# Computing the gate half of the FFN's causal convolution with vector taps instead of banded matmuls

## The reference

```python
def conv_ffn(h, w_up, conv_f_w, w_down):
    u = jnp.einsum("bsd,df->bsf", h, w_up)          # 1024 -> 2 x 2816 channels
    u = causal_dwconv(u, conv_f_w)                  # 3 taps along the sequence, per channel
    gate, val = jnp.split(u, 2, axis=-1)
    return jnp.einsum("bsf,fd->bsd", jax.nn.silu(gate) * val, w_down)
...
for l in range(2):
    h = rmsnorm(x, mix_norm_g[l]);  x = x + token_mixer(h, ...)
    h = rmsnorm(x, ffn_norm_g[l]);  x = x + conv_ffn(h, ...)
return rmsnorm(x, final_norm_g)
```

## Time and profile before

| | |
|---|---|
| two timed runs | 3695.23 and 4191.18 us (median 3943.21) |
| the profiled execution | 3684.81 us, span 3683.8 us on its slowest core |
| spans of the eight cores | 3662.6 to 3683.8 us |
| granted TensorE clock, mean of each core | 0.984 to 0.989 |
| busy share of the span | TensorE 94%, VectorE 51%, ScalarE 28%, GpSimd 17% |

### The profile page before, as it was taken

The page is one execution under the profiler, slowest core; times in us unless marked ns, Lnnn a source line. Parts: engine busy times, 40 slices in busy tenths (PEclk is TensorE's granted clock), DMA queues, the critical chain, the costliest instruction groups (busy, mean ns, idle before and its releaser), DMA issues.

```text
span 3683.8 us, 52643 instructions; the slowest of 8 cores (3662.6 to 3683.8 us)
## 1 busy us (share of the span) xinstructions
PE 3449.2 (94%) x15712; PEld 1534.9 (42%) x15712; DVE 1872.0 (51%) x3110; ACT 1043.6 (28%) x1943; POOL 626.8 (17%) x778
## 2 busy tenths in 40 slices
PE   0888699998999999999999999999999999999997
PEld 0333234443444444444444444444444444444443
DVE  1353233336575566557543333343657566666664
ACT  0322123333232223223213333333323322322321
POOL 2360000001132122123110000000222212211311
PEclk9989999999999999999999999999999999999998
DMA  9859977663454454444446667644444555455454
GB/s 157 267 191 232 180 173 185 179 176 129 155 158 140 153 161 138 151 157 155 140 154 176 176 176 181 175 142 141 130 152 158 162 169 179 140 172 174 156 162 136
DMA packets 148206, 606.76 MB, mean 165 GB/s; under 512 B 14656, under 2 KB 14784, under 8 KB 146976
## 3 DMA queue, kind: packets, MB, share of 16 engines
q1 hardware_dynamic: 130720, 519.49, 44.9%
q0 software_dynamic: 14096, 77.60, 11.2%
q10 hardware_dynamic: 3120, 6.29, 0.7%
HBM read 618.00 MB, written 83.89 MB: 191 GB/s over the span
## 4 chain that ended last, share of the span: by engine, by line
PE 82%; DMA 4%; issue 4%; DVE 4%; ACT 3%; ACTq 2%; another core or an unknown queue 0%; DVEq 0%; SPq 0%
PE ps L270 82%; ACTq L223 2%; DMA ring<-sA 2%; DMA ring<-sCA 2%; ACT stg L475 1%; DVE stg L535 1%; DVE stg L533 1%; DVE stg L481 1%; DVE hbuf L441 0%; ACT stg L537 0%; ACT L527 0%; DVE ps L439 0%; ACT stg L488 0%; DVE xs L571 0%; ACT sd L527 0%
## 5 line engine op out<-in xcount | busy, mean ns | idle before, releaser
L270 PE MATMUL ps<-hbuf,ring 128*128 128x512 bf16 x8192 | 1857.5, 382 | 90.8 <-DVE stg L481 39.4
L270 PE MATMUL ps<-stg,ring 128*128 128x512 bf16 x7072 | 1626.1, 381 | 29.0 <-DMA ring<-sCA 11.5
L270 PEld LDWEIGHTS ps<-hbuf,ring 128*128 128x128 bf16 x8192 | 800.2, 98 | 1087.4 <-issue 151.9
L270 PEld LDWEIGHTS ps<-stg,ring 128*128 128x128 bf16 x7072 | 691.0, 98 | 882.9 <-issue 80.9
L628 POOL TENSOR_TENSOR stg<-stg 128x512 bf16<-128x512 f32 x352 | 446.9, 1269 | 1542.0 <-ACT stg L626 1093.1
L592 ACT ACTIVATE stg<-ps 128x512 bf16<-128x512 f32 x352 | 210.3, 598 | 876.7 <-PE ps L270 876.7
L599 DVE TENSOR_SCALAR stg<-ps,prm_sb 128x512 f32<-128x512 f32 x352 | 264.1, 750 | 311.6 <-PE ps L270 309.8
L626 ACT ACTIVATE stg<-ps 128x512 f32<-128x512 f32 x352 | 210.2, 597 | 525.1 <-PE ps L270 524.1
L481 DVE SCALAR_TENSOR_TENSOR stg<-ps,prm_sb,stg 128x512 bf16<-128x512 f32 x128 | 94.9, 741 | 399.4 <-ACT stg L475 393.1
L602 DVE SCALAR_TENSOR_TENSOR stg<-ps,prm_sb,stg 128x511 f32<-128x511 f32 x352 | 263.8, 749 | 37.4 <-DVE stg L599 0.9
L605 DVE SCALAR_TENSOR_TENSOR stg<-ps,prm_sb,stg 128x510 f32<-128x510 f32 x352 | 263.4, 748 | 38.1 <-DVE stg L602 1.8
(11 more groups left out here) (48 smaller groups left out, 960.6 us busy)
## 6 DMA issues: line engine op xcount, KB each, us to landing
ring<-sU SPq DMA_DIRECT2D x352, 608.0 KB, 4.0
ring<-sD SPq DMA_DIRECT2D x128, 704.0 KB, 4.5
ring<-sA SPq DMA_DIRECT2D x160, 512.0 KB, 5.0
ring<-sCA SPq DMA_DIRECT2D x128, 512.0 KB, 4.2
ring<-sO SPq DMA_DIRECT2D x64, 512.0 KB, 4.0
sU<-wU POOLq DMA_DIRECT2D x22, 1024.0 KB, 12.4
outT<-xs SPq DMA_DIRECT2D x8, 2048.0 KB, 7.7
sD<-wD POOLq DMA_DIRECT2D x8, 1408.0 KB, 14.0
```

The costliest lines, as they stand in the source:

```text
L270: ins = nc.tensor.matmul(ps[:, b, :], lhsT=lhsT, rhs=rhs, start=start, stop=stop)
```

## The change

The gate half is now convolved like the value half. For each of the two banks ScalarE makes the first product (an activation with the tap as its scale, from PSUM to float32 in SBUF), and VectorE does the other two taps, the two halo pieces and the halo copy. Silu runs in place on the gate's result. The three diagonal matmuls per unit, their PSUM bank, the bf16 copy and its halo are gone, and so are both `build_F` with their DMAs; the unit of `sU` shrinks from 2432 to 2048 columns. The gate's result has three buffers, the value's two.

```diff
             build_A(POOL, 1, RFr[:, 0:16384], rfb)
-            build_F(POOL, 0)
             build_B(POOL, 1)
-            build_F(POOL, 1)
             for i in (5, 6, 7):
                 dma(POOL, s_x[i], xt(i), ...)
...
+            def conv_taps(b, acc, accbuf, hl, hlbuf, j, c0):
+                op(ACT, activation(out=acc[:, 0:T], in_=ps[:, b, :], func=AF.Identity, scale=pcol(c0 + 2)), ...)
+                op(DVE, scalar_tensor_tensor(acc[:, 1:T], ps[:, b, 0:T - 1], pcol(c0 + 1), acc[:, 1:T], mult, add), ...)
+                op(DVE, scalar_tensor_tensor(acc[:, 2:T], ps[:, b, 0:T - 2], pcol(c0), acc[:, 2:T], mult, add), ...)
+                op(DVE, scalar_tensor_tensor(acc[:, 0:2], hl[:, j, 0:2], pcol(c0), acc[:, 0:2], mult, add), ...)
+                op(DVE, scalar_tensor_tensor(acc[:, 0:1], hl[:, j, 1:2], pcol(c0 + 1), acc[:, 0:1], mult, add), ...)
+                op(DVE, tensor_copy(hl[:, j, :], ps[:, b, T - 2:T]), ...)
...
             def up(j):
-                slot, sbf = next_unit(sU[..., 0:2432], 2432, [cast_tokens[("U", l, j)], dF])
+                slot, sbf = next_unit(sU[..., 0:2048], 2048, [cast_tokens[("U", l, j)]])
                 ... 16 matmuls into bG, bV ...
-                POOL copies the gate halo, ACT copies ps[bG] to bf16 (L592) and its halo (L594),
-                DVE does TS, STT, STT, STT, STT, COPY on ps[bV] (L599 to L614)
+                kg, kv = j % 3, j % 2
+                conv_taps(bG, accg[kg], accgb[kg], halg, halgb, j, c0)
+                conv_taps(bV, accv[kv], accvb[kv], halv, halvb, j, c0 + 3)
 
             def conv(j):
-                b = alloc_bank()
-                for kt in range(3):
-                    mm(b, slot[:, m0:m0 + 128], ubufs[ui][:, kt:kt + T], kt == 0, kt == 2, ...)
-                op(ACT, activation(out=tmpF[k2], in_=ps[:, b, :], func=AF.Silu), ...)
-                op(POOL, tensor_tensor(out=gbuf[:, j, :], in0=accs[k], in1=tmpF[k2], op=mult), ...)
+                op(ACT, activation(out=accg[kg], in_=accg[kg], func=AF.Silu), ...)
+                op(POOL, tensor_tensor(out=gbuf[:, j, :], in0=accv[kv], in1=accg[kg], op=mult), ...)
```

More of the change, by code:

```diff
@@ L197, in build_program @@
         gbuf = stg[:, o:o + NF * T].rearrange("p (j t) -> p j t", j=NF); o += NF * T
-        ubufs = [stg[:, o + k * 514:o + (k + 1) * 514] for k in range(2)]; o += 2 * 514
-        hal = stg[:, o:o + NF * 2].rearrange("p (j t) -> p j t", t=2); o += NF * 2
-        o = (o + 1) // 2 * 2
+        halg = stg[:, o:o + NF * 4].bitcast(F32).rearrange("p (j t) -> p j t", t=2); o += NF * 4
         halv = stg[:, o:o + NF * 4].bitcast(F32).rearrange("p (j t) -> p j t", t=2); o += NF * 4
-        accs = [stg[:, o + k * 2 * T:o + (k + 1) * 2 * T].bitcast(F32) for k in range(2)]; o += 4 * T
-        tmpF = [stg[:, o + k * 2 * T:o + (k + 1) * 2 * T].bitcast(F32) for k in range(2)]; o += 4 * T
+        accg = [stg[:, o + k * 2 * T:o + (k + 1) * 2 * T].bitcast(F32) for k in range(3)]; o += 6 * T
+        accv = [stg[:, o + k * 2 * T:o + (k + 1) * 2 * T].bitcast(F32) for k in range(2)]; o += 4 * T
         assert o <= 17408, o
@@ L246, in build_program @@
         halvb = [Buf() for _ in range(NF)]
-        accb = [Buf(), Buf()]
+        accgb = [Buf(), Buf(), Buf()]
+        accvb = [Buf(), Buf()]
+        halgb = [Buf() for _ in range(NF)]
         constb = Buf()
@@ L574, in ffn_tile @@
         def ffn_tile(l, i, steps, p2s, tail):
-            dF = dg_tok("F", l)
             units = {}
             steps = list(steps)
+            def conv_taps(b, acc, accbuf, hl, hlbuf, j, c0):
+                op(ACT, lambda: nc.scalar.activation(out=acc[:, 0:T], in_=ps[:, b, :], func=AF.Identity, scale=pcol(c0 + 2)),
+                   reads=[pb[b], prmb], writes=[accbuf])
+                op(DVE, lambda: nc.vector.scalar_tensor_tensor(out=acc[:, 1:T], in0=ps[:, b, 0:T - 1], scalar=pcol(c0 + 1),
+                                                               in1=acc[:, 1:T], op0=ALU.mult, op1=ALU.add),
+                   reads=[pb[b], accbuf, prmb], writes=[accbuf])
+                op(DVE, lambda: nc.vector.scalar_tensor_tensor(out=acc[:, 2:T], in0=ps[:, b, 0:T - 2], scalar=pcol(c0),
+                                                               in1=acc[:, 2:T], op0=ALU.mult, op1=ALU.add),
+                   reads=[pb[b], accbuf, prmb], writes=[accbuf])
+                op(DVE, lambda: nc.vector.scalar_tensor_tensor(out=acc[:, 0:2], in0=hl[:, j, 0:2], scalar=pcol(c0),
+                                                               in1=acc[:, 0:2], op0=ALU.mult, op1=ALU.add),
+                   reads=[hlbuf[j], accbuf, prmb], writes=[accbuf])
+                op(DVE, lambda: nc.vector.scalar_tensor_tensor(out=acc[:, 0:1], in0=hl[:, j, 1:2], scalar=pcol(c0 + 1),
+                                                               in1=acc[:, 0:1], op0=ALU.mult, op1=ALU.add),
+                   reads=[hlbuf[j], accbuf, prmb], writes=[accbuf])
+                op(DVE, lambda: nc.vector.tensor_copy(out=hl[:, j, :], in_=ps[:, b, T - 2:T]),
+                   reads=[pb[b]], writes=[hlbuf[j]])
             def up(j):
-                slot, sbf = next_unit(sU[(l * NF + j) * 128:(l * NF + j + 1) * 128, 0:2432], 2432, [cast_tokens[("U", l, j)], dF])
+                slot, sbf = next_unit(sU[(l * NF + j) * 128:(l * NF + j + 1) * 128, 0:2048], 2048, [cast_tokens[("U", l, j)]])
                 W = slot[:, 0:2048].rearrange("p (c n) -> p c n", c=NCH)
@@ L588, in up @@
                 bG, bV = bks
[L589 to L616, removed]
@@ L618, in conv @@
-            def conv(j):
-                slot, sbf, ui, k = units.pop(j)
-                b = alloc_bank()
-                for kt in range(3):
[L622 to L629, removed]
+                kg, kv = j % 3, j % 2
@@ new lines, in up @@
+                c0 = l * PL + P_CFW + j * 6
+                conv_taps(bG, accg[kg], accgb[kg], halg, halgb, j, c0)
+                conv_taps(bV, accv[kv], accvb[kv], halv, halvb, j, c0 + 3)
+                units[j] = (kg, kv)
+            def conv(j):
+                kg, kv = units.pop(j)
+                op(ACT, lambda: nc.scalar.activation(out=accg[kg][:], in_=accg[kg][:], func=AF.Silu),
+                   reads=[accgb[kg]], writes=[accgb[kg]])
+                op(POOL, lambda: nc.gpsimd.tensor_tensor(out=gbuf[:, j, :], in0=accv[kv][:], in1=accg[kg][:], op=ALU.mult),
+                   reads=[accvb[kv], accgb[kg]], writes=[gfb[j]])
@@ L685, in build_program @@
             else:
-                op(DVE, lambda: nc.vector.memset(hal, 0.0), writes=halb)
+                op(DVE, lambda: nc.vector.memset(halg, 0.0), writes=halgb)
                 op(DVE, lambda: nc.vector.memset(halv, 0.0), writes=halvb)
```

## The result

The changed kernel is slower by 8.2%: the ratio to the kernel before is 1.0821 (95% interval 1.0804 to 1.0837), with times of 3999.4 to 4006.9 us against 3695.2 to 3708.1 us. I forecast +285 us, to 3970, in a range of 3895 to 4085; measured is about +305.

A forecast was written before the change was run, and what follows sets the result against it. VectorE's chain, 2.52 us per bank, was to replace TensorE as the bound of F's unit phase. 3684.8 us before, +329 in F and -43 in the first stage gave 3971, said as 3970 us, range 3895 to 4085.

The forecast's parts named there:

- The chain of 2.52 us: F's unit phase: VectorE's five instructions per bank take 2.50 us plus 0.02 to the next chain; 5.04 us per unit.
- The collision: Start of each F tile: one VectorE halo instruction waits for GpSimd's late product, 0.8 us; later ones miss each other.
- A tile of 151.3 us: One F tile summed step by step from its first matmul: 151.3 us, 21.3 more than before.
- The clock: F's down product: after idle gaps near 5 us TensorE runs partly at 1.2 GHz, 2.2 us per tile; unit phase nothing.
- the rival of a falling clock: F's unit phase: TensorE at 1.2 GHz, up to +660 us, 4630 us; now and then, up to some +100; chance 8%.
- the row of the 2.91 us gap: Evidence against a lower clock in the unit phase: after 2.91 us idle, 16 matmuls took 3.61 us, full speed.
- The first stage: Without both build_F the stage before F gets 43 us shorter: -18 from the stall, -25 from the casts.
- The stall behind the build: First stage: second build_F held VectorE's mixer halo copy 25.09 us, TensorE idle 15.46, then 2.2 slower; removing it gives -18 us.
- the jam of casts: First stage: seven piled-up casts cost TensorE 49 us; an earlier x load saves half, -25 us, bounds 0 and -49.
- The sum: Whole kernel: 3684.8 + 329 (F) - 43 (first stage) = 3971, given as 3970 us.
- The price of 658 ns: Skill's figure for a 512-column PSUM-to-SBUF VectorE instruction; by it a chain of 2.34 us and a kernel near 3843.
- The threshold of 2.04 us: F tile: no slower than before if VectorE's chain per bank is at most 2.04 us; rows give 2.50.

The follow-up runs named there:

- the experiment: Changed kernel with both build_F and their DMAs put back in their old places, output never read: 4025.7 to 4038.3 us, ratio 1.0934 to the kernel before.

## Why the prediction was right, point by point

- **The bound.** TensorE waits for L591 after each group of 8 matmuls. Right, and shown from both sides: less chain gives the time back, more takes it, TensorE work is free.
- **The chain of 2.52 us.** Measured 2.53, and on the timeline some 0.35 us more about once in 12 chains, three times in the tile from 971.15 (the wait of 0.99 us among those of 0.64 above shows such a pause). The cause of this odd pause was not looked for.
- **The collision.** I had 0.8 us per tile for one. In the tile from 971.15 both halo instructions keep their 0.22 us, and the means over the kernel, 221 and 223 ns, leave some 3 us for all 16 tiles, not 13. The odd pauses, 1.1 us in that tile, took the place of this term: the sum held there by luck.
- **A tile of 151.3 us.** Measured 152.3 in the mean of 16 (151 to 154). In the tile from 971.15 the 1.5 us above the sum are 0.2 until the first chain starts (ScalarE's product is 0.69 us, not 0.60), 0.6 in the chains with their odd pauses, 0.2 from the last chain to the down product, and 0.5 in its 155 matmuls. Tiles of the last stage are as long as the others, so its extra matmuls are hidden as forecast.
- **The clock.** 2.2 us per tile forecast. 155 matmuls took 35.0 to 36.6 us against 33.5, in the mean 35.7, and 2.1 to 2.5 us per tile come back when TensorE is kept busy. In the unit phases of the first F stage the granted clock is 1.00, so the rival of a falling clock, and what the Trainium skill (TensorE: Matmul & The Clock Gate, on psum-queue depth-cycling) describes, did not come true there. In the last stage it is 0.97 to 0.98 in four of eight unit phases, and in one of them 16 matmuls took 5.14 us behind idle time of 2.92 us; these tiles are no longer for it, since VectorE bounds them. My argument from the row of the 2.91 us gap was too strong. The trace of the kernel before also has 16 matmuls in 5.15 us behind 2.85 us of idle time, which I did not weigh:

```profile
382.54 5.15 PE L270 MATMUL ps<-hbuf,ring 128*128 128x512 bf16 x16 [2.85 <-DMA ring<-sA]
```

- **The first stage.** -43 forecast, -39 by the means over cores, -25 to -42 by the experiment. The stall behind the build has the forecast size where it occurs (18.39 us idle with the builds, gone without them), but it is not on every core. Of the jam of casts about half stayed: TensorE still waited some 19 us for single units between 240 and 295 us, up to 3.4 us at a time, against 39 us idle before. The two terms were not measured apart.
- **The sum.** On core 5, against the slowest core before, both F stages together are 341 us longer (329 forecast), the first stage is 54 shorter (43 forecast) and the third 5 shorter (nothing forecast); so the +282 of its span is closer to my +285 than its terms are. Of the 33 us by which 4003 lies above 3970, 13 are in the base: the profiled execution before took 3684.8 us, the middle of its timed ones is 3698.
- **The price of 658 ns.** The Trainium skill (VectorE: DVE Perf Modes, section on the TRN2 errata) has this for an instruction of 512 columns: the duration stays at 0.75 us here, but from start to start it is 0.67 where nothing waits, near that figure. My reason for 2.34 us as the chain by that figure was thus wrong in one point: the pauses are no fixed addition, they belong to the order.
- **The threshold of 2.04 us.** I said that a tile is no slower than before up to this chain. No run lies at that point; 1.82 us (half of 3.64) gave a tile of 122.8 us and 2.53 us one of 152.3, against 129.96 before, which is in keeping with it. But I took the chain for fixed ("I see no room"), and this is where the argument was weak: the room was in the pauses.

## What to carry to other kernels

Before work is moved off the busiest engine, add up on the receiving engine what one step there will take from start to start, pauses between dependent instructions included, and compare it with the step that is left: here 2.53 us against 1.73. If it comes out above, look first at the order: two independent chains in turn saved 1.4 of 5.06 us per unit with not one instruction less. And tiny instructions count when they hang on each other: three instructions on one or two columns made 0.8 of the 2.53 us.

## What the runs showed of the hardware

- On VectorE an instruction that reads the result of the one just before it starts 0.85 us after it (0.75 us long), one that doesn't 0.67 us after it. For the instructions on one or two columns it is 0.32 and 0.17 us.
- 43 matmuls without use per tile made the kernel 25 to 38 us faster: behind idle time of 4.46 us the next 155 took 35.54 us (granted clock 0.94), and behind 1.01 us 33.74 (1.00).
- Idle time of 2.85 us was followed by 16 matmuls in 5.15 us and idle time of 2.91 us by 16 in 3.61, in one trace: the gap alone doesn't tell what the clock does.
- A VectorE copy of 120 bf16 columns was held 28.01 us by one GpSimd instruction with both inputs in SBUF, which ended with it. Where the copy started before that instruction it took 0.19 us, which is also the median of the 14 copies.
